# Gated up projections: four products of mixer A, then four of mixer B, over two column tiles

## The chip, the cores and the metric

One core of one Trainium2 chip runs the whole layer. The metric is device time in microseconds of one execution of the kernel, as the median of several runs. The profile comes from one further execution that the hardware profiler recorded.

## What is computed

The reference is one layer of a decoder with two token mixers, A (dilated attention) and B (stick-breaking attention), then attention on a memory and a feed-forward block. The part at issue joins the two mixers:

```
y = (sigmoid(gate_A) * (o_A @ w_up_a) + sigmoid(gate_B) * (o_B @ w_up_b)) @ w_out
h = h + y
```

Sequence and model width are 1024, and o_A and o_B are 512 wide each. Everything is float32.

## The kernel before

All arrays lie transposed: 128 channels on the partitions, 1024 tokens along the free axis, as two halves of 512. An operand of a matmul is split into two fp32r parts, hi (a rounded copy) and lo (what is left of it), and a product is three passes: w_hi with hi, w_hi with lo, w_lo with hi. `passes` (its matmul is line 358) issues them all.

Weights come as a stream of tiles of 128x1024. SyncE loads tile after tile into `stage` (line 314), two buffers. GpSimd splits each in order: `w_hi` (line 324), then `w_lo` (line 326), counted by the semaphore `w_split`. It begins with a tile once `w_begun` says that TensorE has begun the tile after the one that last lay in that buffer. `begin_tile` makes TensorE wait for `w_split`.

The gated stage makes 8 column tiles of 128 channels, j = 0 to 7, in a loop of 4 passes with b = 0, 1 inside. Its moving operand is `n_hi`/`n_lo`: blocks k = 0 to 3 hold mixer A's output, 4 to 7 mixer B's. They come back from memory on ScalarE's DMA queue; ScalarE rounds them (`round_o`, line 901), and VectorE makes the rest (`o_rest`, line 1202), counted by `o_lo_s`. The weight tile of column j holds w_up_a's four blocks and then w_up_b's. Each column tile has four products, c = 0 to 3, of 12 matmuls each: mixer A for both halves, then mixer B for both halves. They go to PSUM banks 0 to 3 in turn, and a product waits (`bank_free`) until the bank that it writes, used four products before, has been read.

For each column tile ScalarE (`gated`, lines 938 to 949) waits for the tile's two gates (`g_in[b]`), takes both sigmoids in place in `g_a[:, b]` and `g_b[:, b]` (line 942, counted by `g_ready`), makes `m_hi` of each half from `y_a` (line 946, after `y_ready`), and then issues the two DMAs that bring the gates of the tile after the next into the same buffer (`load_gates`, line 922).

VectorE reads each product (line 1311), multiplied by its gate: mixer A's into `y_a`, mixer B's into `y_b`. For mixer B's it goes on in the same queue: adds `y_b` to `y_a` (line 1316), waits for ScalarE's `m_hi`, and subtracts it to make `m_lo` (line 1320). `y_a` has four buffers, `y_b` one for each half.

Behind the stage the output projection (`m_hi`/`m_lo` against w_out, two products of 24 matmuls per tile) starts; its first product uses the order (w_hi m_hi, w_lo m_hi, w_hi m_lo) and waits for parts at its first and last block, its second waits for all 16 `m_lo`. Engines execute their queues in order; the order is written out by hand.

Of the kernel before, what the change touches and what calls it, by code (L numbers as in the profile page):

```python
# [17 lines left out]
ALU = mybir.AluOpType  # L18
ACT = mybir.ActivationFunctionType
F32 = mybir.dt.float32  # L20
# [4 lines left out]
P = 128  # L25
T = 1024
D = 1024
KT = D // P
HALF = 512
# [102 lines left out]
def blk(n, size=P):  # L132
    return slice(n * size, (n + 1) * size)


def build(nc, xT, memT, positions, gains, weights, ident_d, rope_d, bias_d, mask_d, outT):
    with ExitStack() as ctx:
# [4 lines left out]
        def sem(name):  # L142
            return ctx.enter_context(nc.semaphore(name))

        def keep(name, shape, dt):
            return ctx.enter_context(nc.sbuf_tensor(name, shape, dt))
# [5 lines left out]
        n_hi = keep("n_hi", [P, KT, T], F32R)  # L152
        n_lo = keep("n_lo", [P, KT, T], F32R)
# [61 lines left out]
        ps = ctx.enter_context(nc.psum_tensor("ps", [P, 8, HALF], F32))  # L215
# [7 lines left out]
        w_rounded, w_split, w_begun = sem("w_rounded"), sem("w_split"), sem("w_begun")  # L223
        bank_full, bank_free = sem("bank_full"), sem("bank_free")
# [14 lines left out]
        o_hi_s, o_lo_s = sem("o_hi_s"), sem("o_lo_s")  # L239
        g_in, g_ready = [sem("g_in0"), sem("g_in1")], sem("g_ready")  # L240
        y_ready, m_hi_s, m_lo_s = sem("y_ready"), sem("m_hi_s"), sem("m_lo_s")
# [17 lines left out]
        B_GATED = B_ROUND + (PAIRS - 1) * BANKS_ROUND + 2 * len(LAST.names)  # L259
# [8 lines left out]
        W_GATED = W_MIX + PAIRS * TILES_IN  # L268
# [9 lines left out]
        def apart(eng):  # L278


            eng.nop(nofuse=True)
# [61 lines left out]
        def _(pe):  # L343
            def passes(bank, units, mv_hi, mv_lo, which, ks, first, last, wait=None):

                n = 0
                total = len(which) * len(ks)
                for p in which:  # L350
                    w = w_lo if p == 2 else w_hi
                    mv = mv_lo if p == 1 else mv_hi
                    for k in ks:
                        if wait and p != 2 and k in (ks[0], ks[-1]):
                            made, count = wait[p]
                            pe.wait_ge(made, count + (k == ks[-1]))
                        b, c = units(k)
                        ins = pe.matmul(bank, w[:, b, c:c + P], mv(k), start=(first and n == 0),  # L358
                                        stop=(last and n == total - 1))
                        if n == 0:  # L360
                            lead = ins
                        n += 1
                return lead, ins

            def begin_tile(number):
                pe.wait_ge(w_split, number)

            def product(bank, b, half, which=(0, 1, 2), hi=None, lo=None, wait=None):

                hi, lo = hi or n_hi, lo or n_lo  # L370
                return passes(bank, lambda k: (b, k * P), lambda k: hi[:, k, blk(half, HALF)],
                              lambda k: lo[:, k, blk(half, HALF)], which, range(KT), which[0] == 0,
                              len(which) == 3 or which[-1] == 2, wait)
# [11 lines left out]
            for t in range(2 * MH):  # L385
# [20 lines left out]
                if t < MH:  # L406
                    lead, last = passes(ps[:, 2 + t, 0:NM], lambda k: (t % 2, k * P), lambda k: mg_hi[:, k, :],
                                        lambda k: mg_lo[:, k, :], (0, 1, 2), range(KT), True, True)
                    last.then_inc(kv_full, 1)
                else:  # L410
                    first = t % 2 == 0
                    for mt in range(2):
                        item = MH + (t - MH) // 2 * 2 + mt
                        n = 0
                        for a, w in ((mg_hi, w_hi), (mg_lo, w_hi), (mg_hi, w_lo)):
                            for k in range(KT // 2):
                                last = pe.matmul(ps[:, 2 + item % 6, 0:NM], a[:, k + (0 if first else KT // 2), blk(mt)],
                                                 w[:, t % 2, blk(k, NM)], start=(first and n == 0),
                                                 stop=(not first and n == 3 * KT // 2 - 1))
                                if mt == 0 and n == 0:  # L420
                                    lead = last
# [114 lines left out]
            pe.wait_ge(o_lo_s, KT // 2)  # L536
            pe.wait_ge(bank_free, B_GATED)
            with pe.Fori(0, KT // 2) as i:
                for b in range(2):
                    begin_tile(i * 2 + (W_GATED + b + 1))  # L540
                    for c in range(4):
                        m, half = c // 2, c % 2
                        n = 4 * b + c
                        if c == 2:
                            pe.wait_ge(o_lo_s, KT)
                        pe.wait_ge(bank_free, i * 8 + (B_GATED + n - 3))
                        lead, last = passes(
                            ps[:, n % 4, :], lambda k: (b, k * P), lambda k: n_hi[:, k, blk(half, HALF)],
                            lambda k: n_lo[:, k, blk(half, HALF)], (0, 1, 2), range(4 * m, 4 * m + 4), True, True)
                        if c == 0:  # L550
                            lead.then_inc(w_begun, 1)
                        last.then_inc(bank_full, 1)


            with pe.Fori(0, KT // 2) as i:
                for b in range(2):
                    begin_tile(i * 2 + (W_OUT + b + 1))
                    for half in range(2):
                        n = 2 * b + half
                        pe.wait_ge(bank_free, i * 4 + (B_OUT + n - 3))  # L560
                        if n == 0:
                            lead, last = product(ps[:, n, :], b, half, (0, 2, 1), m_hi, m_lo,
                                                 ((m_hi_s, 2 * KT - 2), (m_lo_s, 2 * KT - 2)))
                        else:
                            pe.wait_ge(m_lo_s, 2 * KT)
                            lead, last = product(ps[:, n, :], b, half, hi=m_hi, lo=m_lo)
# [25 lines left out]
            for s in range(MU + 3):  # L592
# [21 lines left out]
                if 0 <= u < MU:  # L614
# [6 lines left out]
                    n = 0  # L621
# [11 lines left out]
            with pe.Fori(0, KT // 4) as i:  # L633
                for b in range(2):
                    begin_tile(i * 2 + (W_OM + b + 1))
                    for c in range(4):
                        n = 4 * b + c
                        pe.wait_ge(bank_free, i * 8 + (B_OM + n - 3))
                        lead, last = passes(
                            ps[:, n % 4, :], lambda k: (b, (4 * (c // 2) + k) * P),  # L640
                            lambda k: qm_hi[:, k, blk(c % 2, HALF)], lambda k: qm_lo[:, k, blk(c % 2, HALF)],
                            (0, 1, 2), range(4), True, True)
# [59 lines left out]
            for c in range(4):  # L702
                pe.wait_ge(bank_free, B_END + c - 3)
                lead, _ = last_down(c, (0,), False)
# [3 lines left out]
            for c in range(2 * KT):  # L708
                if c < 4:
                    _, last = last_down(c, (1,), True)  # L710
                else:
# [3 lines left out]
                    lead, last = last_down(c, range(2), True)  # L715
# [9 lines left out]
        def _(act):  # L725
# [212 lines left out]
            def gated(i, more):  # L938
                for b in range(2):
                    act.wait_ge(g_in[b], i * 32 + 32)  # L940
                    for g in (g_a, g_b):
                        act.activation(g[:, b, :], g[:, b, :], ACT.Sigmoid).then_inc(g_ready, 1)
                    for half in range(2):
                        act.wait_ge(y_ready, i * 4 + (2 * b + half + 1))
                        apart(act)
                        act.activation(m_hi[:, bass.ds(i * 2 + b, 1), blk(half, HALF)].rearrange("p o n -> p (o n)"),
                                       y_a[:, 2 * b + half, :], ACT.Copy).then_inc(m_hi_s, 1)
                    if more:
                        load_gates(i * 2 + (b + 2), b)

            with act.Fori(0, KT // 2 - 1) as i:
                gated(i, True)
            gated(KT // 2 - 1, False)


# [34 lines left out]
            for s in range(MU + 4):  # L990
                if s < MU:
                    act.wait_ge(mx_ready, s + 1)
                    for j in range(2):
                        c = 2 * (s % 2) + j
# [49 lines left out]
            for c in range(2 * KT):  # L1044
                half, j = divmod(c, KT)
# [15 lines left out]
        def _(dve):  # L1061
# [8 lines left out]
            def flat(ap):  # L1070
                return ap.rearrange("p o n -> p (o n)")
# [228 lines left out]
                return t[:, j, :] if isinstance(j, int) else flat(t[:, bass.ds(j, 1), :])  # L1300

            with dve.Fori(0, KT // 2) as i:
                for b in range(2):
                    j = i * 2 + b
                    dve.wait_ge(g_ready, i * 4 + (2 * b + 2))
                    for c in range(4):
                        m, half = c // 2, c % 2
                        n = 4 * b + c
                        ya, yb = y_a[:, 2 * b + half, :], y_b[:, half, :]
                        dve.wait_ge(bank_full, i * 8 + (B_GATED + n + 1))  # L1310
                        dve.tensor_tensor((ya, yb)[m], ps[:, n % 4, :], (g_a, g_b)[m][:, b, blk(half, HALF)], ALU.mult
                                          ).then_inc(bank_free, 1)
                        if m == 0:
                            continue
                        dve.wait_ge(bank_free, i * 8 + (B_GATED + n + 1))
                        dve.tensor_tensor(ya, ya, yb, ALU.add).then_inc(y_ready, 1)
                        dve.wait_ge(m_hi_s, i * 4 + (2 * b + half + 1))
                        hi = flat(m_hi[:, bass.ds(j, 1), blk(half, HALF)])
                        lo = flat(m_lo[:, bass.ds(j, 1), blk(half, HALF)])
                        dve.tensor_tensor(lo, ya, hi.bitcast(F32), ALU.subtract).then_inc(m_lo_s, 1)  # L1320


            def add_product(j, bank, start):
# [54 lines left out]
            for s in range(MU + 4):  # L1378
                t = s // HU + 1
                if s < MU:  # L1380
                    c = slice(2 * (s % 2), 2 * (s % 2) + 2)
# [6 lines left out]
                if 0 <= u < MU:  # L1388
                    c = 2 * (u % 2)
# [174 lines left out]
```

## Time and profile before

| | |
|---|---|
| timed runs | 1957.56, 1957.62, 1952.74 us; median 1957.56 |
| the profiled execution | 1952.04 us, its span 1949.9 us |
| TensorE matmuls busy | 1835.7 us, 94% of the span, 8578 of them |
| VectorE busy | 1121.2 us, 58% |
| ScalarE busy | 601.7 us, 31% |
| GpSimd busy | 537.6 us, 28% |
| granted TensorE clock, mean | 0.979 |
| chain that ended last | TensorE 73%, VectorE 16% |

Span is the time from the first to the last recorded event of the core; the execution's own time is 2.1 us longer. The gated stage runs from about 870 to 961 us of the span. The share of busy time is that of all stages together, so the views of this stretch alone have to be read for the change.

### The profile page before, as it was taken

The page shows a single profiled execution, that of the slowest core. Times are in us where ns is not written, and L with a number is a line of the kernel's source. Part 1 is how long each engine was busy: PE and PEld are TensorE (multiplying, and loading weights), DVE is VectorE, ACT ScalarE, POOL GpSimd, SP SyncE. Part 2 cuts the span into 40 slices and gives each one's busy share as a digit, 9 for nine tenths or more (in the row PEclk, how much of TensorE's full clock was granted, in tenths as well). Part 3 has the DMA queues.
Part 4 walks back from the last instruction along what each step waited for, and adds up shares of the span by engine and source line. Part 5 has one row for each costly group of instructions (what it writes and reads, how often), then busy time and mean ns, then how long its engine had stood idle before and what let it go on. Part 6 is the DMA issues. An engine that isn't in the chain of part 4 may idle for free.

```text
span 1949.9 us, 24701 instructions
## 1 busy us (share of the span) xinstructions
PE 1835.7 (94%) x8578; PEld 1475.8 (76%) x8578; DVE 1121.2 (58%) x1684; ACT 601.7 (31%) x1024; POOL 537.6 (28%) x296
## 2 busy tenths in 40 slices
PE   5699999999999999969999889999999999999995
PEld 5577777777777777757887767888888888888884
DVE  8547894788478957986544565333333433343336
ACT  3324852485247525763212333000000000000003
POOL 5321112111211220213332112333333333333335
PEclk9899999999999999979999989999999999999998
DMA  5311111111111110145312001111111111111112
GB/s 218 101 36 39 38 45 61 40 38 44 61 40 38 44 60 29 49 168 197 119 52 89 22 18 48 43 45 53 43 54 43 54 43 53 43 43 54 43 43 86
DMA packets 43238, 118.71 MB, mean 61 GB/s; under 512 B 6160, under 2 KB 14608, under 8 KB 43024
## 3 DMA queue, kind: packets, MB, share of 16 engines
q1 hardware_dynamic: 21312, 75.66, 11.6%
q10 hardware_dynamic: 21840, 41.96, 6.4%
q8 instruction: 48, 0.79, 0.2%
q14 instruction: 38, 0.31, 0.1%
HBM read 97.67 MB, written 18.87 MB: 60 GB/s over the span
## 4 chain that ended last, share of the span: by engine, by line
PE 73%; DVE 16%; issue 5%; ACT 4%; ACTq 1%; DMA 1%; DVEq 0%; POOL 0%; SPq 0%; POOLq 0%
PE ps L358 63%; PE ps L472 4%; DVE e_row L1260 4%; DVE e_row L1259 2%; PE ps L503 2%; PE ps L488 2%; DVE pt L1244 1%; DVE rms L1125 1%; ACT pt L843 1%; DVE raw L1158 1%; ACTq L801 1%; DVE h L1469 1%; DVE raw L1174 1%; ACT n_hi L969 0%; DVE h L1329 0%
## 5 line engine op out<-in xcount | busy, mean ns | idle before, releaser
L324 POOL TENSOR_SCALAR w_hi<-w_stage 128x1024 fp32r<-128x1024 f32 x138 | 149.9, 1086 | 1380.2 <-issue 686.2
L358 PE MATMUL ps<-n_hi,w_hi 128*128 128x512 f32 x1536 | 396.2, 398 | 27.2 <-DVE raw L1158 16.2
L358 PE MATMUL ps<-n_lo,w_hi 128*128 128x512 f32 x1536 | 389.9, 395 | 0.0
L358 PE MATMUL ps<-n_hi,w_lo 128*128 128x512 f32 x1536 | 387.9, 393 | 0.0
L326 POOL TENSOR_TENSOR w_lo<-w_stage,w_hi 128x1024 fp32r<-128x1024 f32 x138 | 366.4, 2655 | 11.5
L358 PEld LDWEIGHTS ps<-n_hi,w_hi 128*128 128x128 f32 x1536 | 285.8, 190 | 94.5 <-DVE raw L1158 22.6
L358 PEld LDWEIGHTS ps<-n_lo,w_hi 128*128 128x128 f32 x1536 | 287.9, 190 | 60.0
L358 PEld LDWEIGHTS ps<-n_hi,w_lo 128*128 128x128 f32 x1536 | 285.3, 188 | 58.1
L1329 DVE TENSOR_TENSOR h<-ps,h 128x512 f32<-128x512 f32 (+1 forms) x192 | 132.0, 690 | 156.9 <-PE ps L358 156.5
L1024 ACT ACTIVATE a_hi<-u_f 128x1024 fp32r<-128x1024 f32 x22 | 23.4, 1062 | 475.4 <-DVE u_f L1435 475.4
L1427 DVE TENSOR_TENSOR u_f<-ps,rms 128x512 f32<-128x512 f32 x44 | 30.4, 691 | 205.3 <-PE ps L358 205.3
L843 ACT ACTIVATE pt<-ps 128x128 fp32r<-128x128 f32 (+7 forms) x128 | 83.4, 652 | 186.2 <-PE ps L488 185.0
L472 PE MATMUL ps<-qk 64*128 64x512 f32 (+3 forms) x576 | 138.0, 363 | 1.5 <-issue 1.3
L472 PEld LDWEIGHTS ps<-qk 64*128 64x128 f32 x576 | 92.2, 185 | 55.2 <-issue 43.2
L358 PE MATMUL ps<-a_hi,w_hi 128*128 128x512 f32 x352 | 112.4, 398 | 3.0 <-DVE a_lo L1437 3.0
L358 PE MATMUL ps<-a_lo,w_hi 128*128 128x512 f32 x352 | 111.8, 396 | 0.0
L358 PE MATMUL ps<-a_hi,w_lo 128*128 128x512 f32 x352 | 111.8, 396 | 0.0
L1225 DVE CUSTOM_DVE_ANT_0 rows<-ps,bias_A 128x128 f32<-128x128 f32 (+7 forms) x64 | 48.4, 756 | 104.9 <-PE ps L472 99.7
L1244 DVE TENSOR_TENSOR pt<-ps,pt 128x128 fp32r<-128x128 f32 (+7 forms) x128 | 96.2, 752 | 19.0 <-ACT pt L843 17.7
L1260 DVE TENSOR_TENSOR_SCAN e_row<-e_row 128x1024 f32<-128x1024 f32 (+7 forms) x64 | 101.7, 1589 | 2.2
L1427 DVE TENSOR_TENSOR g_f<-ps,rms 128x512 f32<-128x512 f32 x44 | 30.0, 684 | 96.1 <-PE ps L358 93.9
L488 PE MATMUL ps<-ident,rows 128*128 128x128 f32 x576 | 84.4, 274 | 0.0
(168 smaller groups left out, 2221.4 us busy)
## 6 DMA issues: line engine op xcount, KB each, us to landing
w_stage<-weights_in SPq DMA_DIRECT2D x138, 512.0 KB, 3.3
gates_scratch<-raw ACTq DMA_DIRECT2D x16, 512.0 KB, 2.8
o_scratch<-o_sum ACTq DMA_DIRECT2D x128, 32.0 KB, 1.8
n_lo<-o_scratch ACTq DMA_DIRECT2D x8, 512.0 KB, 5.0
g_a<-gates_scratch ACTq DMA_DIRECT2D x8, 512.0 KB, 3.7
g_b<-gates_scratch ACTq DMA_DIRECT2D x8, 512.0 KB, 4.5
h<-x_t_in ACTq DMA_DIRECT2D x8, 512.0 KB, 9.0
out_t<-h ACTq DMA_DIRECT2D x16, 256.0 KB, 2.1
```

What stands on the lines that cost most here:

```text
L324: pool.tensor_scalar(w_hi[:, b, :], stage[:, b, :], 1.0, 1.0, ALU.mult, ALU.mult).then_inc(w_rounded, 1)
L326: pool.tensor_tensor(w_lo[:, b, :], stage[:, b, :], w_hi[:, b, :].bitcast(F32), ALU.subtract).then_inc(w_split, 1)
L358: ins = pe.matmul(bank, w[:, b, c:c + P], mv(k), start=(first and n == 0), stop=(last and n == total - 1))
L472: ins = pe.matmul(ps[:, 2 + c // HALF, 0:w], a[hs, blk(qb)], b[hs, c:c + w], start=(n == 0), stop=(n == 2 and not diagonal))
L488: ins = pe.transpose(ps_t[:, blk(kb)], rows[:, u % 4, blk(kb)], ident[:])
L503: ins = pe.matmul(ps[:, 6 + u % 2, 0:2 * P], v[:, kb, hd, :, :].rearrange("p a d -> p (a d)"), pt[:, kb, :, :].rearrange("p a q -> p (a q) ...
L843: act.activation(pt[:, 0:width // P, 0, :], ps_t[:, 0:width].rearrange("p (n q) -> p n q", q=P), ACT.Copy).then_inc(pt_hi_s, 1)
L1225: dve.tensor_tensor_reduce(out=row, in0=ps_rows[:, 0:width], in1=bias_A[:, T - width:T], scale=1.0, scalar=NEG_MAX, op0=ALU.add, op1=ALU.m ...
L1244: dve.tensor_tensor(pt[:, 0:nb, 1, :], ps_t[:, 0:width].rearrange("p (n q) -> p n q", q=P), pt[:, 0:nb, 0, :].bitcast(F32), ALU.subtract). ...
L1260: link(dve.tensor_tensor_scan(e[:, ::-1], e[:, ::-1], e[:, ::-1], 0.0, ALU.add, ALU.bypass))
L1329: dve.tensor_tensor(hj, ps[:, bank + half, :], hj, ALU.add).then_inc(bank_free, 1)
L1427: dve.tensor_tensor(dst[:, blk(half, HALF)], ps[:, bank + half, :], rms[:, blk(half, HALF)], ALU.mult).then_inc(bank_free, 1)
```

## The change

TensorE, ScalarE and VectorE change their order of the same work; what is computed, its operations and its DMAs are the same. One pass of the loop takes eight products in one sequence, n = 0 to 7, in which m (the mixer) is n // 4, b (the column tile of the pass) n // 2 % 2 and half n % 2. Both weight tiles of a pass are therefore in use nearly through all of it: the second is first needed at n = 2, and the first is given back at n = 6. The wait for mixer B's low parts stands before n = 4. ScalarE waits for the gates of both tiles, takes the sigmoids of g_a for both and then of g_b for both, and then makes the four `m_hi`. Its loads stay behind the `m_hi` of their tile.

```diff
             with pe.Fori(0, KT // 2) as i:
-                for b in range(2):
-                    begin_tile(i * 2 + (W_GATED + b + 1))
-                    for c in range(4):
-                        m, half = c // 2, c % 2
-                        n = 4 * b + c
-                        if c == 2:
-                            pe.wait_ge(o_lo_s, KT)
-                        pe.wait_ge(bank_free, i * 8 + (B_GATED + n - 3))
...
-                        if c == 0:
-                            lead.then_inc(w_begun, 1)
-                        last.then_inc(bank_full, 1)
+                for n in range(8):
+                    m, b, half = n // 4, n // 2 % 2, n % 2
+                    if m == 0 and half == 0:
+                        begin_tile(i * 2 + (W_GATED + b + 1))
+                    if n == 4:
+                        pe.wait_ge(o_lo_s, KT)
+                    pe.wait_ge(bank_free, i * 8 + (B_GATED + n - 3))
...
+                    if half == 0 and b == m:
+                        lead.then_inc(w_begun, 1)
+                    last.then_inc(bank_full, 1)
...
             def gated(i, more):
                 for b in range(2):
                     act.wait_ge(g_in[b], i * 32 + 32)
-                    for g in (g_a, g_b):
+                for g in (g_a, g_b):
+                    for b in range(2):
                         act.activation(g[:, b, :], g[:, b, :], ACT.Sigmoid).then_inc(g_ready, 1)
+                for b in range(2):
                     for half in range(2):
                         act.wait_ge(y_ready, i * 4 + (2 * b + half + 1))
...
             with dve.Fori(0, KT // 2) as i:
-                for b in range(2):
+                for n in range(8):
+                    m, b, half = n // 4, n // 2 % 2, n % 2
                     j = i * 2 + b
-                    dve.wait_ge(g_ready, i * 4 + (2 * b + 2))
-                    for c in range(4):
-                        m, half = c // 2, c % 2
-                        n = 4 * b + c
...
+                    if half == 0:
+                        dve.wait_ge(g_ready, i * 4 + (n // 2 + 1))
+                    ya, yb = y_a[:, 2 * b + half, :], y_b[:, half, :]
+                    if n == 3:
+                        dve.wait_ge(bank_free, i * 8 + (B_GATED + n))
+                    dve.wait_ge(bank_full, i * 8 + (B_GATED + n + 1))
```

The rest of VectorE's body is unchanged, one level of indentation less.

## Rows read from the trace of the kernel before

**Rows 1.** Chain that ended last, in time: start us, us, engine, tile, line, count.

```profile
879.57 171.53 PE ps L358 x744
```

**Rows 2.** Windows view, gated stage: us, busy PE, PEld, DVE, ACT, POOL, clock, DMA.

```profile
879.57:962.00 82.43, 82.43 (x363) 68.24 (x364) 50.99 (x62) 23.50 (x30) 26.54 (x15) 1.00 0.42 151
```

**Rows 3.** Timeline, TensorE, products 0 to 4: start us, us, work, idle before it.

```profile
870.49 2.07 PE L358 MATMUL ps<-n_hi,w_hi 128*128 128x512 f32 x4 [5.49 <-DVE n_lo L1202]
...
877.22 1.07 PE L358 MATMUL ps<-n_hi,w_lo 128*128 128x512 f32 x4
879.57 1.19 PE L358 MATMUL ps<-n_hi,w_hi 128*128 128x512 f32 x4 [1.28 <-DVE n_lo L1202]
...
882.44 1.07 PE L358 MATMUL ps<-n_hi,w_hi 128*128 128x512 f32 x4
...
885.16 1.07 PE L358 MATMUL ps<-n_hi,w_hi 128*128 128x512 f32 x4
```

**Rows 4.** Timeline, the second tile's split; page, loads of weights (median us to landing).

```profile
872.56 2.40 POOL L326 TENSOR_TENSOR w_lo<-w_stage,w_hi 128x1024 fp32r<-128x1024 f32 x1
...
w_stage<-weights_in SPq DMA_DIRECT2D x138, 512.0 KB, 3.3
```

**Rows 5.** Timeline, VectorE, ScalarE and GpSimd, products 2 and 3.

```profile
882.64 0.69 DVE L1311 TENSOR_TENSOR y_b<-ps,g_b 128x512 f32<-128x512 f32 x1 [1.59 <-PE ps L358]
...
883.36 0.69 DVE L1316 TENSOR_TENSOR y_a<-y_a,y_b 128x512 f32<-128x512 f32 x1
...
884.24 0.63 ACT L946 ACTIVATE m_hi<-y_a 128x512 f32 x1 [4.61 <-DVE y_a L1316]
...
885.05 0.69 DVE L1320 TENSOR_TENSOR m_lo<-y_a,m_hi 128x512 f32 x1 [1.00 <-ACT m_hi L946]
...
885.66 0.68 DVE L1311 TENSOR_TENSOR y_b<-ps,g_b 128x512 f32<-128x512 f32 x1
885.71 1.05 POOL L324 TENSOR_SCALAR w_hi<-w_stage 128x1024 fp32r<-128x1024 f32 x1 [10.75 <-PE ps L358]
...
886.38 0.92 DVE L1316 TENSOR_TENSOR y_a<-y_a,y_b 128x512 f32<-128x512 f32 x1
...
886.84 2.72 POOL L326 TENSOR_TENSOR w_lo<-w_stage,w_hi 128x1024 fp32r<-128x1024 f32 x1
...
887.47 0.63 ACT L946 ACTIVATE m_hi<-y_a 128x512 f32 x1 [2.59 <-DVE y_a L1316]
...
888.14 0.34 ACTq L922 DMA_DIRECT2D g_b<-gates_scratch  x1
888.27 1.84 DVE L1320 TENSOR_TENSOR m_lo<-y_a,m_hi 128x512 f32 x1 [0.97 <-ACT m_hi L946]
...
889.49 1.04 ACT L942 ACTIVATE g_b<-g_b 128x1024 f32<-128x1024 f32 x1
...
890.65 1.29 DVE L1311 TENSOR_TENSOR y_a<-ps,g_a 128x512 f32<-128x512 f32 x2 [0.54 <-ACT g_b L942]
```

**Rows 6.** Views of lines 1311 and 324: count, min/median/max ns, first and last start.

```profile
L1311 DVE TENSOR_TENSOR y_b<-ps,g_b x16: 681/686/692, 882.6 to 961.7; 128x512 f32<-128x512 f32 x16
...
L324 POOL TENSOR_SCALAR w_hi<-w_stage x138: 1043/1052/1560, 12.4 to 1904.1; 128x1024 fp32r<-128x1024 f32 x138
```

**Rows 7.** View of tile g_b: its loads and their landing.

```profile
DMA to landing us min/median/max: 4.3/4.5/7.8
```

**Rows 8.** Timeline, TensorE, output projection, end of its first product and its second.

```profile
965.05 2.03 PE L358 MATMUL ps<-m_lo,w_hi 128*128 128x512 f32 x8
966.92 2.03 PE L358 MATMUL ps<-m_hi,w_hi 128*128 128x512 f32 x8
```

**Rows 9.** TensorE's timeline behind 2.37 and 3.05 us of wait; window, columns as rows 2.

```profile
74.26 2.08 PE L358 MATMUL ps<-n_hi,w_hi 128*128 128x512 f32 x8 [2.37 <-DVE rms L1144]
...
1909.60 0.80 PE L358 MATMUL ps<-a_hi,w_hi 128*128 128x512 f32 x1 [3.05 <-DVE a_lo L1437]
...
1910.00:1915.00 5.00, 5.00 (x18) 3.93 (x18) 3.38 (x5) 1.90 (x3) 2.07 (x2) 0.75 0.00 0
```

More of the change, by code:

```diff
@@ L538, in _ @@
             with pe.Fori(0, KT // 2) as i:
-                for b in range(2):
-                    begin_tile(i * 2 + (W_GATED + b + 1))
-                    for c in range(4):
-                        m, half = c // 2, c % 2
-                        n = 4 * b + c
-                        if c == 2:
-                            pe.wait_ge(o_lo_s, KT)
-                        pe.wait_ge(bank_free, i * 8 + (B_GATED + n - 3))
-                        lead, last = passes(
-                            ps[:, n % 4, :], lambda k: (b, k * P), lambda k: n_hi[:, k, blk(half, HALF)],
-                            lambda k: n_lo[:, k, blk(half, HALF)], (0, 1, 2), range(4 * m, 4 * m + 4), True, True)
-                        if c == 0:
-                            lead.then_inc(w_begun, 1)
-                        last.then_inc(bank_full, 1)
+                for n in range(8):
[5 more added lines that the diff above has]
+                    pe.wait_ge(bank_free, i * 8 + (B_GATED + n - 3))
+                    lead, last = passes(
+                        ps[:, n % 4, :], lambda k: (b, k * P), lambda k: n_hi[:, k, blk(half, HALF)],
+                        lambda k: n_lo[:, k, blk(half, HALF)], (0, 1, 2), range(4 * m, 4 * m + 4), True, True)
+                    if half == 0 and b == m:
+                        lead.then_inc(w_begun, 1)
+                    last.then_inc(bank_full, 1)
             with pe.Fori(0, KT // 2) as i:
@@ L1302, in _ @@
             with dve.Fori(0, KT // 2) as i:
-                for b in range(2):
+                for n in range(8):
+                    m, b, half = n // 4, n // 2 % 2, n % 2
                     j = i * 2 + b
-                    dve.wait_ge(g_ready, i * 4 + (2 * b + 2))
-                    for c in range(4):
-                        m, half = c // 2, c % 2
-                        n = 4 * b + c
[L1309 to L1320, printed above, removed]
@@ new lines, in _ @@
+                    if half == 0:
[4 more added lines that the diff above has]
+                    dve.wait_ge(bank_full, i * 8 + (B_GATED + n + 1))
+                    dve.tensor_tensor((ya, yb)[m], ps[:, n % 4, :], (g_a, g_b)[m][:, b, blk(half, HALF)], ALU.mult
+                                      ).then_inc(bank_free, 1)
@@ new lines, in _ @@
+                    if m == 0:
+                        continue
+                    dve.wait_ge(bank_free, i * 8 + (B_GATED + n + 1))
+                    dve.tensor_tensor(ya, ya, yb, ALU.add).then_inc(y_ready, 1)
+                    dve.wait_ge(m_hi_s, i * 4 + (2 * b + half + 1))
+                    hi = flat(m_hi[:, bass.ds(j, 1), blk(half, HALF)])
+                    lo = flat(m_lo[:, bass.ds(j, 1), blk(half, HALF)])
+                    dve.tensor_tensor(lo, ya, hi.bitcast(F32), ALU.subtract).then_inc(m_lo_s, 1)
```

## The prediction

> **What bounds the kernel now.** I read the chain that ended last first: from 879.57 us a single row of 171.53 us of TensorE products carries it through the gated stage and on into the next one [rows 1]. So only two things count in this stage: a moment in which TensorE stands still, and work added to TensorE. The windows view says that TensorE was busy 82.43 of 82.43 us there at a granted clock of 1.00 [rows 2], so the stage has no waits except at its head. TensorE's own timeline shows that head [rows 3]: product 0 starts at 870.49, the row of 877.22 is the last third of product 1, and the next row starts at 879.57 after a wait of 1.28 us for n_lo. From 882.44 to 885.16 lies product 3 alone, so a product takes 2.72 us and a third of one 0.907. Product 1 ends therefore at 878.13, product 2 starts at 879.57 and product 3 at 882.44, 2.87 later (refilling costs 0.15). What is waited for is mixer B's low part, the last n_lo of VectorE.
>
> I number products 0 to 7 in one pass of the loop, and write s8 for the start of the next pass.
>
> **What the change removes.** Four products of mixer A come first, 4 x 2.72 from s0. Product 2 needs the second weight tile at 878.13; GpSimd made it by 874.96 [rows 4]. Product 4, the first of mixer B, would start at 870.49 to 878.13 plus 2 x 2.72 = 883.57, four us after n_lo was there (879.57). The wait goes: 879.57 - 878.13 + 0.15 = 1.59 us gained, once. No matmul is added or removed.
>
> **What it moves, weight tiles.** The split of tile 2i+1 starts on GpSimd 0.55 after the pass begins (885.16 to 885.71) and ends at 889.56, 4.40 after it [rows 3, 5]. It was wanted 10.88 later, now 5.44 later, since product 2 uses it. The same holds for the tile of the next pass, released at product 6. Slack 1.04 us, and what VectorE can add to one split is about 0.4 (below). I take nothing; if that cover goes, each 0.1 us over 1.04 is paid up to 7 times. SyncE's loads into stage are issued behind the splits, at s0 - 1.04 and s0 + 4.40, and are wanted at s6 + 0.55 and s8 + 0.55, 17 us later each, where a load takes 3.3 [rows 4].
>
> **What it moves, VectorE.** A product of mixer A costs VectorE one read, 0.69. A product of mixer B costs a chain [rows 5]: read at 882.64, addition 883.36, ScalarE's m_hi 884.24, m_lo 885.05, next read 885.66, a period of 3.02 us with VectorE waiting inside it. With A and B in alternation, two such chains (6.04) and two reads (1.4) stand against 10.88. Now four chains in a row, 12.1 us, stand against four products, 10.88; that alone would leave VectorE 0.9 us behind after three of them. But the second chain of the rows is longer: its addition takes 0.92 and its m_lo 1.84 instead of 0.69, and GpSimd's w_lo 2.72 instead of 2.40 [rows 4, 5]. The m_lo issued at 888.27 ends 0.55 after w_lo (889.56). So an instruction of VectorE with both inputs in SBUF and one of GpSimd run one after the other. The read, one input in PSUM, is never long: 681 to 692 ns in 16 [rows 6]. GpSimd's w_hi can be made to wait as well: median 1052, longest 1560 ns [rows 6].
>
> The Trainium skill, page "GPSIMD Engine Reference", section 1 (Specifications), says the SBUF interfaces are shared with VectorE, with contention for VectorE instructions that have two SBUF inputs. By that rule the read of product 7 may run beside a split, which is the lower end of my sum below; if it could not, only the upper end would be left. The rows above agree beside w_hi; none shows a read of this stage beside w_lo.
>
> Before, one split per 10.88 us met one chain of two. Now both splits of a pass fall into the row of four chains, at s6 + 0.55 and s8 + 0.55. Walking through, with s4 = 883.57, s6 = 889.01, s8 = 894.45, 2.72 apart for each product, the distances of rows 5 between the steps, and a read 0.20 behind TensorE's end (882.44 to 882.64) [rows 3, 5]:
> - product 4: read 886.49, m_lo ends 889.59, next read 889.51.
> - product 5: addition 890.23 waits for w_hi (889.56 to 890.61), ends 891.17. w_lo runs until 893.43. m_lo, ready to start at 892.17, ends 893.98.
> - product 6: read 893.90, addition ends 895.31, holding up w_hi of the next split (issued 895.00) until 896.3. m_lo is issued at 896.31, w_lo at 896.32: a photo finish. If w_lo wins, m_lo ends at 899.25; if m_lo wins, it ends at 897.00 and the next addition is what waits, until 899.82.
> - product 7: addition ends at 900.56 (w_lo first) or 899.82 (m_lo first).
>
> Then the loads. The gate loads of tile 2i+3 are issued behind m_hi of product 7; in the rows g_b is issued 0.84 after the end of the addition (887.30 to 888.14) [rows 5], and lands 4.3 to 7.8 us, median 4.5, later [rows 7]. The change makes ScalarE wait for both tiles' gates before its first sigmoid, so all four sigmoids of a pass stand behind this last load; before, the load had a whole tile's time to land. With 4.4 us: 900.56 + 0.84 + 4.4 = 905.8. Sigmoid 1.04, VectorE 0.12 behind it (889.49 + 1.04 to 890.65), read 0.69 [rows 5]: with 0.1 from landing to sigmoid and 0.12 from read to TensorE (my estimates, from that 0.12), bank 0 is free at 907.75 and TensorE goes on at 907.87. Product 12 was due at 894.45 + 4 x 2.72 = 905.33: a stall of 2.54, with refilling 2.69. With m_lo first 0.74 less, 1.95. The path runs from product 5's end through VectorE, GpSimd, ScalarE and a DMA back to TensorE, so the stall doesn't use itself up; it comes at each of the 3 passes after the first: 8.1 or 5.9 us. The gates of the first tile of a pass are loaded behind product 5, some 9 us sooner, and hold nobody up.
>
> **The end of the stage.** The output projection's second product waits for all 16 m_lo. Before, there was no stall: the third row of its first product begins at 965.05, its second product 1.87 later, straight on [rows 8], so a product there takes 3 x 1.87 = 5.60. Now the last product 7's m_lo ends 7.80 (or 7.06) after the start of the output projection, plus 0.13 to TensorE; the second product is due at 5.60. Stall 2.3 or 1.6; the 15th m_hi, wanted 1.6 after the start and ready at 1.7, adds 0.1. Nothing of it comes back, TensorE being the bound behind it.
>
> **Sum.** -1.6 + 8.1 + 2.3 + 0.1 = +8.9 us, or -1.6 + 5.9 + 1.6 + 0.1 = +6.0. I take the middle, +7.5. The profiled execution took 1952.0 us (span 1949.9), so it would read 1959.5. Of the three timed runs two stand at 1957.6 and one at 1952.7; against the median, 1957.56, the sum gives 1965.
>
> **Rivals.**
> (a) The clock falls. After TensorE waited 3.05 us at 1909.60, the granted clock of 1910 to 1915 is 0.75: half of it at the lower level, 1.2 GHz, so 2.5 us in which 1.25 were lost. After 2.37 us at 74.26 it was not: eight matmuls in 2.08 [rows 9]. The new stalls, 2.0 to 2.7, lie nearer the second. If the clock falls in two to four of them, +2.5 to +5 on top: 1967.5 to 1970.
> (b) Not slower. If VectorE and GpSimd miss each other, the four chains are 3.02 each: product 7 is read at 895.55, its addition ends 896.96, g_b lands at 902.2, bank 0 is free at 904.2, before 905.33. No stall in the loop, and the last m_lo ends 4.2 into the output projection, before 5.6. What is left is the gain: -1.6 us, 1956. The point at which it turns is 905.33: the addition of product 7 has to end by 898.0. Against it: two splits of 3.5 us of GpSimd's time cannot both be missed in a row of 12 us; the second chain of the rows pays in every tile.
> (c) Partly so: the gates land sooner than the 4.3 that is the least in the rows, since no weight load is on its way beside them now, m_lo comes first, and VectorE's queue is a few tenths shorter in each pass than I have it. The stalls shrink to some 1 us each: +2 to +5, 1960 to 1962.
> (d) The second weight tile is late. Were GpSimd held up for 1.04 more than in the rows, the stalls would be at products 0 and 2; in my walk it is 0.4. This lies inside the range.
>
> **Numbers.** Forecast 1965, of 0.55, split 0.42 above and 0.13 below 5.9 us more; (a) 0.13; (b) 0.14; (c) 0.13; something faster that I don't see 0.05. A measurement tells 0.3%, 5.9 us, from no change: slower 0.55, same 0.40, faster 0.05. The range holds (c), both ends of the sum and two lost clocks, and (b) only against the median: 1956.5 to 1971.
>
> **What would show it.** In the changed profile: TensorE's row of n_lo's wait at 879.57 gone; three new waits of 2 to 2.7 us, one per pass, at product 4, put down to VectorE's y_a; a fourth of about 2 at the output projection's second product, for m_lo; ScalarE idle some 4 us before g_a's first sigmoid; additions and m_lo of products 5 to 7 long. Wrong is the walk if the waits are at product 2 (weight tiles), and rival (b) holds if there are none.

## The result and the profile after

The changed kernel takes 1967.65 us (median of 5, 1966.16 to 1969.4), the kernel before 1956.65 (median of 5): a ratio of 1.0069, interval 1.0051 to 1.0088. By the medians it is 11 us slower, by the ratio 13.5; a time of 1965 and slower was forecast. The profiled execution is the one of 1967.65 us.

| | before | after |
|---|---|---|
| profiled execution, its own time | 1952.04 us | 1967.65 us |
| span | 1949.9 us | 1965.5 us |
| first product of the gated stage starts | 870.49 | 873.88 |
| output projection's second product starts | 966.92 | 981.65 |
| the stretch between the two | 96.43 | 107.77 |
| from there to the end of the span | 983.0 | 983.9 |

So 11.3 of the span's 15.6 us lie in the stage. The 3.4 us ahead of it and the 0.9 behind it are in code that the change doesn't touch; two more profiles of the kernel before, under experiment 0, show how far these parts scatter. TensorE's waits, after (us in total, times, longest):

```profile
PE ps L358 <- DVE y_a L1313: 8.2, 3, 3.0
PE ps L358 <- DVE n_lo L1203: 5.5, 1, 5.5
PE ps L358 <- DVE m_lo L1322: 1.1, 1, 1.1
```

The second row is the wait ahead of the first product, as in [rows 3]; the 1.28 us behind product 1 are gone. In their place stand three waits for a bank and one at the output projection. TensorE's timeline (start us, us, work, idle before it):

```profile
873.88 2.07 PE L358 MATMUL ps<-n_hi,w_hi 128*128 128x512 f32 x4 [5.50 <-DVE n_lo L1203]
...
882.33 1.07 PE L358 MATMUL ps<-n_hi,w_hi 128*128 128x512 f32 x4
...
908.62 1.07 PE L358 MATMUL ps<-n_hi,w_lo 128*128 128x512 f32 x4
912.50 1.21 PE L358 MATMUL ps<-n_hi,w_hi 128*128 128x512 f32 x4 [2.81 <-DVE y_a L1313]
...
937.58 1.66 PE L358 MATMUL ps<-n_hi,w_hi 128*128 128x512 f32 x4 [2.98 <-DVE y_a L1313]
939.03 1.91 PE L358 MATMUL ps<-n_lo,w_hi 128*128 128x512 f32 x4
940.73 1.45 PE L358 MATMUL ps<-n_hi,w_lo 128*128 128x512 f32 x4
942.02 1.09 PE L358 MATMUL ps<-n_hi,w_hi 128*128 128x512 f32 x4
...
963.69 1.19 PE L358 MATMUL ps<-n_hi,w_hi 128*128 128x512 f32 x4 [2.44 <-DVE y_a L1313]
...
974.71 2.11 PE L358 MATMUL ps<-m_hi,w_hi 128*128 128x512 f32 x8
...
981.65 2.09 PE L358 MATMUL ps<-m_hi,w_hi 128*128 128x512 f32 x8 [1.10 <-DVE m_lo L1322]
```

Each wait stands at product 4 of a pass. Behind the second one the product takes 4.44 us (937.58 to 942.02) instead of 2.89 (912.50 to 915.39, behind the first): the granted clock was at its lower level for a while, and that cost 1.55. The windows view shows it (columns as rows 2):

```profile
910.00:915.00 5.00, 2.50 (x11) 2.05 (x12) 2.58 (x4) 3.90 (x4) 0.00 (x0) 1.00 0.00 1
935.00:940.00 5.00, 2.42 (x7) 1.94 (x8) 2.58 (x4) 3.90 (x4) 0.00 (x0) 0.81 0.00 1
940.00:945.00 5.00, 5.00 (x20) 4.03 (x19) 1.76 (x3) 0.63 (x1) 0.00 (x0) 0.85 0.00 0
```

From product 5's addition on to the first wait's end, the engines other than TensorE (timeline of after):

```profile
894.43 0.92 DVE L1318 TENSOR_TENSOR y_a<-y_a,y_b 128x512 f32<-128x512 f32 x1
894.89 2.72 POOL L326 TENSOR_TENSOR w_lo<-w_stage,w_hi 128x1024 fp32r<-128x1024 f32 x1
...
896.32 1.84 DVE L1322 TENSOR_TENSOR m_lo<-y_a,m_hi 128x512 f32 x1 [0.97 <-ACT m_hi L947]
897.78 6.14 SPq L314 DMA_DIRECT2D w_stage<-weights_in  x2
898.08 0.68 DVE L1313 TENSOR_TENSOR y_b<-ps,g_b 128x512 f32<-128x512 f32 x1
898.79 0.69 DVE L1318 TENSOR_TENSOR y_a<-y_a,y_b 128x512 f32<-128x512 f32 x1
899.19 1.22 POOL L324 TENSOR_SCALAR w_hi<-w_stage 128x1024 fp32r<-128x1024 f32 x1 [1.58 <-issue]
...
900.47 0.69 DVE L1322 TENSOR_TENSOR m_lo<-y_a,m_hi 128x512 f32 x1 [0.98 <-ACT m_hi L947]
900.49 2.93 POOL L326 TENSOR_TENSOR w_lo<-w_stage,w_hi 128x1024 fp32r<-128x1024 f32 x1
901.08 0.68 DVE L1313 TENSOR_TENSOR y_b<-ps,g_b 128x512 f32<-128x512 f32 x1
901.80 2.17 DVE L1318 TENSOR_TENSOR y_a<-y_a,y_b 128x512 f32<-128x512 f32 x1
...
904.80 0.34 ACTq L921 DMA_DIRECT2D g_b<-gates_scratch  x1
...
910.56 2.00 ACT L942 ACTIVATE g_a<-g_a 128x1024 f32<-128x1024 f32 x2 [5.79 <-DMA g_b<-gates_scratch]
911.75 2.70 DVE L1313 TENSOR_TENSOR y_a<-ps,g_a 128x512 f32<-128x512 f32 x4 [6.13 <-ACT g_a L942]
```

This is the ring, as the experiments call it: VectorE's last addition of a pass, the gate load behind it, the sigmoid, VectorE's read that frees the bank. m_lo of product 6 was issued 0.02 us ahead of w_lo and won; product 7's addition then stood behind w_lo and took 2.17 us. The gate load went out at 904.80, the sigmoid began 5.76 later, the bank was read at 911.75, and TensorE went on at 912.50.

### The profile page after: what moved, and what is told of

It reads as the page before. It is cut to its first block, busy times and chain, and to the rows that moved or that the text cites. A ratio compares the mean times of both kernels' runs of the same rounds, so it can differ in the third digit from the quotient of the medians.

```text
span 1965.5 us, 24705 instructions
## 1 busy us (share of the span) xinstructions
PE 1840.6 (94%) x8578; PEld 1477.2 (75%) x8578; DVE 1119.0 (57%) x1684; ACT 601.2 (31%) x1024; POOL 539.1 (27%) x296
## 4 chain that ended last, share of the span: by engine, by line
PE 68%; DVE 17%; issue 5%; ACT 5%; ACTq 2%; DMA 1%; POOL 1%; DVEq 0%; SPq 0%; POOLq 0%
PE ps L358 58%; PE ps L472 4%; DVE e_row L1261 4%; DVE e_row L1260 2%; PE ps L503 2%; PE ps L488 2%; DVE pt L1245 1%; DVE y_a L1318 1%; DVE rms L1126 1%; ACT pt L842 1%; DVE raw L1159 1%; DMA g_b<-gates_scratch 1%; POOL rms L339 1%; ACTq L800 1%; DVE h L1471 1%
## 5 line engine op out<-in xcount | busy, mean ns | idle before, releaser
L358 PE MATMUL ps<-n_hi,w_hi 128*128 128x512 f32 x1536 | 401.9, 403 | 34.8 <-DVE raw L1159 16.8
L326 POOL TENSOR_TENSOR w_lo<-w_stage,w_hi 128x1024 fp32r<-128x1024 f32 x138 | 367.5, 2663 | 11.5
```

What stands on the lines that cost most here:

```text
L326: pool.tensor_tensor(w_lo[:, b, :], stage[:, b, :], w_hi[:, b, :].bitcast(F32), ALU.subtract).then_inc(w_split, 1)
```

## Experiments

Edits are against the changed kernel, and `...` stands for lines left out; times are ratios to the kernel before, taken on the same chip. "Stage" is the stretch from the first product to the output projection's second, 96.43 before.

**0. The change again, and the kernel before again.** No edit.

> The change unaltered, a second look. In its first profile the three waits for bank 0 were 2.81, 2.98 and 2.44 us, and the clock fell behind the second alone, which cost some 1.6 us. My theory (a loop through VectorE's chain, the second tile's gate load and the sigmoid): three waits again, 2.2 to 3.2 us each, 8 to 9 in all, and about 1.1 at the output projection; 9 to 12 us over the kernel before. Rival (the waits were made by chance, a slow load or the clock): waits that differ by more than 1 us from those of the first profile, or one missing. If the fallen clock is not tied to one place, it comes behind another wait or behind none.

Measured: 1.0059 (1.0044 to 1.0074), stage 107.22. Waits, in the order of time:

```profile
908.97 1.85 PE L358 MATMUL ps<-n_hi,w_hi 128*128 128x512 f32 x4 [2.57 <-DVE y_a L1313]
...
935.13 1.20 PE L358 MATMUL ps<-n_hi,w_hi 128*128 128x512 f32 x4 [2.51 <-DVE y_a L1313]
...
961.30 1.20 PE L358 MATMUL ps<-n_hi,w_hi 128*128 128x512 f32 x4 [2.48 <-DVE y_a L1313]
...
979.28 2.10 PE L358 MATMUL ps<-m_hi,w_hi 128*128 128x512 f32 x8 [1.11 <-DVE m_lo L1322]
```

Same places, same sizes within 0.5 us. The clock fell behind the first wait this time (1.85 for its row), and behind the second as well, one row late: from 935.13 to 961.30 lie 26.17 us, where eight products (21.76), one delay (2.48 + 0.16, see below) and one refilling (0.17) make 24.57. Each fall cost some 1.6.

> The kernel before, a second profile. Behind the stage (from the output projection's second product to the end) its first profile had 983.0 us; eight profiles of changed kernels had 983.9 to 987.4. If that is the clock's luck behind the stage, this one lies at 984 to 987; if every changed kernel costs something behind the stage, it stays within 1 us of 983. The stage itself: 96.4 within 1 us.

> The kernel before, a third profile, for the same question: stage 96.4 within 1 us; behind it 983 (a cost of the change) or 984 to 987 (luck).

Measured: one execution each. Stages 96.39 and 96.42; behind the stage 981.1 and 986.0, and ahead of it 868.48 and 874.03. The first fits neither expected answer, the second the one called luck. So what lies outside the stage scatters by some 5 us on either side in the unchanged kernel. Ahead of the stage the clock isn't the only cause: one wait of TensorE near the start (60 us, for r_col) took 11.85, 7.51 and 10.41 us in the three profiles. Behind it a part is the clock's. From the mean before the memory attention to the one behind it three profiles of the kernel before took 150.5, 152.2 and 154.0; granted clock in its first 50 us, in the shortest and the longest (windows view, columns as rows 2):

```profile
1068.00:1118.00 50.00, 43.53 (x247) 36.89 (x247) 29.24 (x69) 17.94 (x57) 6.96 (x4) 1.00 0.09 31
```

```profile
1074.00:1124.00 50.00, 44.53 (x239) 37.67 (x238) 27.61 (x68) 17.93 (x57) 6.92 (x4) 0.93 0.09 29
```

The ten profiles of changed kernels (the change twice and every experiment below) took 153.6 to 155.5 there. All lie above two of the three of before, four above the third too. That may be luck or may not; experiment 3 comes back to it, and it isn't settled.

**1. A wait for each tile's gates.**

```diff
...
-                for b in range(2):
-                    act.wait_ge(g_in[b], i * 32 + 32)
                 for g in (g_a, g_b):
                     for b in range(2):
+                        if g is g_a:
+                            act.wait_ge(g_in[b], i * 32 + 32)
...
```

> The change, but ScalarE waits for a tile's gates only ahead of that tile's own sigmoid, so the first tile's g_a is ready while the second's load is still on its way. Theory A (the wait for both loads ahead of the first sigmoid holds bank 0): VectorE reads product 0 of the next pass some 0.2 us behind a sigmoid that starts right behind the load's issue (905.2 on the clock of the first profile), at 906.5 instead of 911.75; the bank is free 2.3 us ahead of need; no wait in the loop. Left are the gain of 1.6 and a wait of 1 to 2 us at the output projection: 0 to 1 us from the kernel before, 8 to 11 below the change. Theory B (VectorE is simply too slow with four chains in a row, whatever the sigmoids do): the waits stay, at product 4 or later, over 1.5 us each.

Measured: 1.0020 (1.0008 to 1.0033), some 7.6 us under the change, stage 98.42. All three waits for a bank are gone. So the place of ScalarE's wait turned the late load into a TensorE stall: theory A holds, B falls. But the output projection's waits came to 2.2 us instead of 1 to 2, and the time is 3.9 us over the kernel before instead of 0 to 1, of which the stage has 2.0:

```profile
963.24 1.87 PE L358 MATMUL ps<-m_hi,w_hi 128*128 128x512 f32 x7 [0.21 <-ACT m_hi L947]
966.22 0.50 PE L358 MATMUL ps<-m_hi,w_hi 128*128 128x512 f32 x1 [1.11 <-ACT m_hi L947]
...
971.29 2.10 PE L358 MATMUL ps<-m_hi,w_hi 128*128 128x512 f32 x8 [0.84 <-DVE m_lo L1322]
```

**2. Short w_lo.** For tiles 48 to 57 GpSimd makes 128 of 1024 columns of w_lo and leaves the rest out; cols is 128 for these tiles and 1024 for all others.

```diff
...
-                pool.tensor_tensor(w_lo[:, b, :], stage[:, b, :], w_hi[:, b, :].bitcast(F32),
+                pool.tensor_tensor(w_lo[:, b, 0:cols], stage[:, b, 0:cols], w_hi[:, b, 0:cols].bitcast(F32),
...
```

> The change, but for weight tiles 48 to 57 (the gated stage's and two of the output projection) GpSimd makes only 128 of 1024 columns of w_lo, so the rest of w_lo is left out there; every other instruction stays. w_lo falls from 2.4 to some 0.4 us. Theory (VectorE's chain is stretched by sharing with GpSimd): the additions and m_lo of products 5 to 7 fall to 0.69 to 1.1 each, the addition of product 7 ends near 2.5 to 3.5 us into the next pass instead of 6.1, the gates land 2.5 to 4 sooner, and the three waits vanish or fall under 0.5; no wait at the output projection. Rival (four chains in a row are too long by themselves, 12.1 against 10.9 us, and sharing adds little): the waits fall by under 1 us each. If a weight load beside the gates' is what made them land after 5.7 instead of 4.4 us, they land after 4.5 here.

Measured: one execution, stage 101.41. Waits 2.03, 0.77 and 1.48 (4.3 in sum, against 8.2 and 7.6 of the change), the clock fell behind the first, and there was no wait at the output projection. The timeline, engines other than TensorE:

```profile
896.37 48.89 SPq L314 DMA_DIRECT2D w_stage<-weights_in  x5
896.51 0.69 DVE L1320 TENSOR_TENSOR y_a<-y_a,y_b 128x512 f32<-128x512 f32 x1
...
898.02 0.34 ACTq L923 DMA_DIRECT2D g_b<-gates_scratch  x1
...
904.88 2.00 ACT L944 ACTIVATE g_a<-g_a 128x1024 f32<-128x1024 f32 x2 [6.88 <-DMA g_b<-gates_scratch]
```

Product 7's addition took 0.69 again instead of 2.17 and ended at 897.2. But the waits did not vanish, as the theory had it: the shorter split let the weight load start at 896.37, 1.15 us ahead of the gate loads, and the sigmoid began 6.9 us behind the issue of g_b; in the next two passes, with the same 1.15, it was 5.6 and 6.3 (5.4 to 5.9 in the change). The 4.5 that I expected came in none. The stretched chain is one part of the wait; another is the load.

**3. The first pass alone in the new order.** TensorE, ScalarE and VectorE take pass 0 as in the change, passes 1 to 3 in the order before (with one wait for a sigmoid ahead of the products that use it). ScalarE waits for each tile's gates by itself in all passes, as in experiment 1.

> Only the first of the four passes takes A's four products first; the other three alternate as before. If the gain of 1.6 us at the head is separate from the price (theory), the wait of 1.3 for n_lo is gone, there is no wait in the loop and none at the output projection: 1.6 us faster than the kernel before, which a measurement here may not tell from none. Rival (the first pass's late gates still hold a bank): one wait of 1 to 3 us behind the first pass, so 0 to 1.5 slower.

> The kernel with only the first pass in the new order once more. Its stage was 2.2 us shorter in the profile (94.2 against 96.4 us from the first product to the output projection's second), its time the same as before's (0.03% over, interval -0.07 to 0.14%). If the gain of the head is real in the time too, 1 to 2.5 us faster here; if something behind the stage takes it back, within 1 us.

Measured: 1.0003 (0.9993 to 1.0014) and 1.0002 (0.9991 to 1.0013), stage 94.21 and 94.29. No wait is left in the stage, and it is 2.2 us shorter than before; the time doesn't show it, and both intervals (-1.4 to 2.7 us and -1.8 to 2.5) leave a gain of 2.2 out. The two profiles had 985.4 us behind the stage, those of before 981.1, 983.0 and 986.0. The same shows in all eight timed comparisons of this document: a changed kernel's time stands 0.4 to 2.8 us, 1.6 in the mean, further above the kernel before than its stage does in the profile. So something outside the stage seems to take back a part of the gain. No experiment isolates it, and what it is stays open.

**4. Weight loads later.** SyncE issues the loads of weight tiles 53, 55 and 57 only behind the first sigmoid of passes 1, 2 and 3.

```diff
...
+                        if lo == first and b == 1:
+                            sp.wait_ge(g_ready, i * 4 + (5 - 4 * first))
                         src = weights[bass.ds(i * 2 + b, 1), :, :].rearrange("o p n -> p (o n)")
...
```

> The change, but SyncE issues the loads of weight tiles 53, 55 and 57 only behind the first sigmoid of the pass that follows the split that freed their buffer, so that no weight load runs beside the late gate loads of a pass. Theory (the gate loads landed 5.4 to 5.8 us after their issue instead of 4.4 because a weight load ran beside them): the three landings fall to 4.3 to 4.7, and each wait for bank 0 by the same 1.0 to 1.3, to 1.2 to 1.8 us; 3 to 4 us less than the change. Rival (two loads of ScalarE's own queue take that long when nothing else runs): landings over 5.2, waits as before.

Measured: 1.0040 (1.0027 to 1.0054), some 3.7 us less than the change, stage 102.91. Waits 1.58, 1.82 and 1.53 (the clock fell behind the second), the landing in the view of g_b (min/median/max) as in [rows 7], and the first of the three loads:

```profile
DMA to landing us min/median/max: 4.3/4.4/7.3
```

```profile
898.61 0.34 ACTq L925 DMA_DIRECT2D g_b<-gates_scratch  x1
...
903.15 2.00 ACT L946 ACTIVATE g_a<-g_a 128x1024 f32<-128x1024 f32 x2 [4.56 <-DMA g_b<-gates_scratch]
```

The sigmoid began 4.54 behind the issue here, the 4.5 of the sum, and 4.77 and 4.51 in the next two passes. The weight load beside the gate loads is what had stretched them.

**5. Both parts away.** Experiments 2 and 4 together.

> Short w_lo (128 of 1024 columns for tiles 48 to 57, the rest left out) and the later weight loads together. With the short w_lo alone the waits were 2.03, 0.77 and 1.48 us, and the gates landed 6.8, 5.4 and 6.2 us behind their issue. If the change's wait is the sum of two parts, VectorE's chain stretched by GpSimd and the landing stretched by the weight load, then with both gone the gates land after 4.3 to 4.7 and no wait is left in the loop. If a wait of over 0.5 is left, a third part is missing.

Measured: one execution. TensorE waits for nothing from 874 on in the stage, which takes 94.31 us. Two causes, the chain stretched by GpSimd and the load stretched by the weight load, make up the whole wait, given that ScalarE waits for both loads in one place; no third is missing.

**6. Eight banks.**

```diff
-                    pe.wait_ge(bank_free, i * 8 + (B_GATED + n - 3))
+                    pe.wait_ge(bank_free, i * 8 + (B_GATED + n - 7))
```

with the products in banks 0 to 7.

> The change with its products in eight PSUM banks instead of four, so that TensorE may run eight products ahead of VectorE's reads. Theory (what is late is the ring VectorE, gate load, sigmoid, VectorE, 24.4 us long against 21.8 of products; the bank only passes it on): the three waits in the loop go, VectorE falls behind by some 2.6 us more in each pass, and the lag comes back at the output projection as waits for m_hi and m_lo, 8 to 10 us in sum; the time is that of the change within 2 us. Rival (the banks are the bound): no waits anywhere but 1.1 at the output projection, 8 us less than the change.

Measured: 1.0019 (1.0005 to 1.0034), stage 99.69: between the two. The waits in the loop are gone and lag comes back at the output projection, as the ring theory says, but less than half of what it gave:

```profile
963.48 3.83 PE L358 MATMUL ps<-m_hi,w_hi 128*128 128x512 f32 x8 [2.81 <-ACT m_hi L947]
...
971.58 2.09 PE L358 MATMUL ps<-m_hi,w_hi 128*128 128x512 f32 x8 [0.53 <-DVE m_lo L1322]
```

The ring got shorter once TensorE no longer waited in it: the first sigmoids of the passes start at 908.03, 930.60 and 953.48, 22.7 apart, where the change has 910.56, 935.63 and 961.75, 25.6 apart. With VectorE lagging, its row of chains and TensorE's release of the tiles no longer fall together: product 7's addition took 0.69 in two passes, and in these two the sigmoid began 4.5 behind the gates' issue, with the weight load 3.7 us and more ahead; in the first pass, where that addition took 2.17 and a weight load went out 0.7 ahead, it was 6.65. My theory had held the ring's length fixed; it depends on where the splits fall in it.

**7. Both remedies that keep all the work.** Experiments 1 and 4 together.

> The change with ScalarE's wait for each tile's gates only ahead of its own sigmoid and with the three weight loads moved later. The first alone left 2.2 us of waits at the output projection, where I had expected 1 to 2. Theory: there VectorE began the last row of four chains late, because the second tile's gates landed late; with landings of 4.4 us the chains start in time, the output projection's waits fall to some 1.1 to 1.5, none in the loop, and the time is 1 to 3 us above the kernel before. Rival: the four chains beside two splits set the end whenever they start, so 2 us or more of waits stay.

Measured: 0.9999 (0.9986 to 1.0012), stage 95.52. The only wait is 1.11 at the output projection, so the extra of experiment 1 was the late landing:

```profile
964.37 2.09 PE L362 MATMUL ps<-m_hi,w_hi 128*128 128x512 f32 x8 [1.11 <-DVE m_lo L1326]
```

This version keeps the order of the change and costs what the kernel before costs. None of the versions beats it.

## Why the prediction was right

**The head.** Forecast 1.59 gained. The wait went, but the gain isn't that difference. In all three profiles of before the third product starts 9.08 or 9.09 us behind the first, whatever the clock did: the wait was 1.28, 1.22 and 0.52, the last where the clock rose later. In changed kernels it starts 6.9 to 8.5 behind the first, as the clock rises. So the wait for n_lo had hidden the slow start in part, and without it 0.6 us (after, 8.45) to 2.1 (experiment 0, 6.97) are gained, and 0.15 for product 2's refilling.

**Weight tiles.** Forecast free: true, TensorE waits for no w_lo in the stage in any run. The split wanted most ended at 903.42, and product 2 of that pass started at 904.09 (908.62 + 0.91 less two products): 0.7 to spare.

**VectorE's chain.** The walk held step by step. Counted from the start of the next pass (898.65 here, 909.53 less four products), product 7's addition was to end at 5.37 (m_lo first) or 6.11; it ended at 5.32. The photo finish was one: 900.47 against 900.49, 925.37 against 925.39, 952.04 against 952.06, m_lo first each time. The load followed 0.83 later (0.84 forecast), and from the sigmoid's start to TensorE's 1.94 (1.97 forecast).

**The load: the term that was mis-sized.** I took 4.4 us and 0.1 to the sigmoid; it took 5.76, 5.93 and 5.39. The reason given in rival (c), that no weight load is beside them now, was the opposite of what happened. SyncE's load was put behind the split, at s0 + 4.40, with up to 0.4 of delay for the split: at s8 + 4.8 for the next pass. The gate loads of the walk go out at s8 + 5.7 and 6.2. It went out at 903.59, s8 + 4.9:

```profile
903.59 0.33 SPq L314 DMA_DIRECT2D w_stage<-weights_in  x1
```

Both numbers were in my text; I never laid them side by side. Experiment 4 puts the price at 0.7 to 1.2 per wait, 3.7 us in all by the ratios 1.0059 and 1.0040, whose difference alone lies hardly clear of noise; the waits and landings of the two traces carry this reading.

**The sum of the stalls.** Forecast 5.9 with m_lo first, refilling included. TensorE's delay is 0.16 more than the wait that the view shows (909.53, where product 4 was due, to 912.50 are 2.97, against 2.81), so the three come to 2.97, 3.14 and 2.60, with 3 x 0.17 of refilling 9.2. The surplus of 3.3 is the load: 1.26, 1.43 and 0.89 over my 4.5, 3.6 in sum. In experiment 0 the delays and refilling make 8.5.

**The end.** Forecast 1.6 (m_lo first), measured 1.10 + 0.16. The last m_lo ended 6.80 behind the output projection's start, not 7.06: behind the loop the steps from VectorE to ScalarE are about 0.1 shorter, as in the last pass of before.

**Rival (a), the clock.** It was half of the truth. It fell behind one of the three waits in one profile of the change and behind two in the other, 1.6 us each. In the stage it fell, over all runs, behind waits of 2.98, 2.81 (experiment 6), 2.57, 2.51, 2.03 and 1.82 us and not behind 2.81 (after), 2.48, 2.44, 1.58, 1.53 and 1.48. The length of one wait didn't decide it, and my reading of [rows 9], that stalls of 2.0 to 2.7 lie nearer the one without a fall, was wrong. With it the stage adds up: the head -0.63 and -0.15 for product 2's refilling, delays +9.2, clock +1.55, the end +1.26 and a slower row +0.07 make 11.3, as measured; in experiment 0, -2.26 + 8.5 + 3.1 + 1.3 + 0.1 = 10.7 against 10.8.

**Rivals (b) to (d).** (b) would have been the case with GpSimd out of the way, but its splits fell into the row of chains as forecast. Experiment 5 has no wait, as (b) says, but only with the weight load moved as well. (c) and (d) didn't happen.

**The signs.** Three waits at product 4 and a fourth at the output projection came as listed, but two of the three were longer than 2.7 (2.81 and 2.98), the fourth was 1.10 instead of about 2, and ScalarE idled 5.8 us instead of 4.

**Luck.** The path and the places were right; that 1965 lay so near 1967.65 is in part luck. The load and the clock were too small in my sum, and the m_lo-first case, the true one, stood 1.5 us under my middle, so taking the middle made good a part of it. The base of 1957.56 was 0.9 above the median of five, 1956.65. The increase itself was forecast as 7.5 and measured as 11.0 by the medians, 13.5 by the ratio, and some 2 us of the latter lie outside the stage, where my sum has nothing.

## What to carry to other kernels

An order that gathers one engine's cheap steps at one end of a pass gathers its dear ones at the other; walk the dear row against every engine that shares a path with it, and against the loads that this row releases. Lay all issue times of one stretch in a single line, the DMAs of all queues too: a transfer that had landed in time came 0.9 to 2.4 us later here once another one was issued 0.7 to 1.15 us ahead of it. And a wait for two loads in one place makes the first buffer as late as the second, which here cost some 7.6 of 11.5 us (the ratios 1.0059 and 1.0020).

## What the runs showed of the hardware

- VectorE's instruction with two SBUF inputs and GpSimd's take turns in either direction: w_hi 1.22 instead of 1.05 behind an addition, an addition 2.17 instead of 0.69 behind w_lo, m_lo ahead of w_lo by 0.02 us keeping its 0.69. VectorE's reads with one input in PSUM stayed at 678 to 692 ns beside w_lo too (901.08). The Trainium skill, "GPSIMD Engine Reference", section 1 (Specifications), names VectorE's instructions with two SBUF inputs among those that contend with GpSimd. By that rule the lower end of the sum was open, and the trace agrees.
- Two loads of 512 KB from one queue: the sigmoid that waits for both began 4.3 to 4.8 us behind the second's issue when no weight load had been issued in the 3.6 us ahead of the first (experiments 4 to 7). With a third load of 512 KB issued 0.7 us ahead of the first it was 5.4 to 5.9 in eight cases (the change, experiments 0 and 1) and 6.65 in one (experiment 6), with 1.15 us it was 5.6, 6.3 and 6.9 (experiment 2), with 2.0 us 4.9 (experiment 1, third pass).
- The clock fell behind TensorE's waits of 1.82 to 2.98 us six times and stayed up behind others of 1.48 to 2.81 six times; a fall cost 1.6 us where rows allow a sum; the length of the wait alone doesn't say which.
- A stall that ends at a fixed time hides a slow clock ahead of it: the third product came 9.08 or 9.09 us behind the first in three profiles with three different clocks.
